# A fused decoder layer on one core: the last two modulation blocks move behind the attention pairs, and the page products start with the first pair

## The reference

```
mod = silu(c) @ w_ada + b_ada -> shift, scale, gate     (w_ada is 1024 x 3072)
h   = rms_norm(x) * (1 + scale) + shift
z   = h @ w_in                                          (1024 x 8200, 64 column tiles of 128)
A:  prompt: causal attention, 8 heads x 64, over z's q, k, v
    sample: 16 pages x 128 cached keys; mean key of each block of 2 pages,
            best 3 of 8 blocks by q . mean(k), softmax over those keys and the new one
B:  mLSTM, 4 heads, prompt and samples
u = sigmoid(ga) * (A * silu(za)) @ w_att + sigmoid(gm) * (B * silu(zm)) @ w_mlstm
y = rms_norm(x + gate * (u @ w_out))
```

## Time and profile before

| | |
|---|---|
| median of three runs | 740.91 us |
| the profiled execution | 738.85 us, its span 737.1 us |
| PE busy | 686.6 us, 93% |
| DVE busy | 480.9 us, 65% |
| POOL busy | 435.9 us, 59% |
| ACT busy | 333.4 us, 45% |
| mean granted TensorE clock | 0.973 of 2.4 GHz |
| loaded and stored | 144.72 MB, mean 196 GB/s |

### The profile page before, as it was taken

One profiled execution on the slowest core, in us unless ns is written; L12 is line 12 of the kernel. 1 busy time (PEld: TensorE's weight loads), 2 busy tenths in 40 slices (PEclk: granted clock), 3 DMA queues, 4 the chain that ended last, 5 costly groups with the idle time before them and its releaser, 6 DMA issues.

```text
span 737.1 us, 14735 instructions
## 1 busy us (share of the span) xinstructions
PE 686.6 (93%) x5012; PEld 610.7 (83%) x5012; DVE 480.9 (65%) x482; ACT 333.4 (45%) x727; POOL 435.9 (59%) x278
## 2 busy tenths in 40 slices
PE   2899999998998979999999999999899999999996
PEld 0575888786877948988999999997789998999974
DVE  0540689998999974895697687761665349444435
ACT  5544474646364325563464545612422224332643
POOL 4211257685686515899679688761495557666520
PEclk9998899999999988999999999999899999999999
DMA  8977858988798761286777567757548355732202
GB/s 315 343 269 233 242 177 244 280 256 270 231 305 262 222 220 29 70 253 198 226 212 228 186 197 238 215 180 207 140 114 228 100 154 174 238 109 85 87 25 92
DMA packets 156904, 144.72 MB, mean 196 GB/s; under 512 B 7547, under 2 KB 115152, under 8 KB 156852
## 3 DMA queue, kind: packets, MB, share of 16 engines
q1 hardware_dynamic: 142984, 137.15, 61.6%
q10 hardware_dynamic: 13876, 7.02, 3.1%
HBM read 135.10 MB, written 9.11 MB: 196 GB/s over the span
## 4 chain that ended last, share of the span: by engine, by line
PE 56%; DVE 16%; issue 10%; POOL 6%; SPq 5%; DMA 4%; ACT 3%; DVEq 0%; POOLq 0%; ACTq 0%
PE ps L553 39%; DVE sb_arenaA L1822 4%; PE ps L983 3%; POOL sb_wL L1507 3%; SPq L398 2%; DVE sb_arenaA L1969 2%; SPq L399 2%; POOL sb_arenaA L1553 2%; DVE sb_arenaA L1826 2%; POOL sb_arenaA L1585 1%; PE ps L822 1%; DMA sb_arenaA<-in_cache_k 1%; PE ps L783 1%; DVE sb_arenaB L1969 1%; DMA sb_arenaB<-in_x_sample 1%
## 5 line engine op out<-in xcount | busy, mean ns | idle before, releaser
L1507 POOL TENSOR_TENSOR sb_wL<-sb_wraw,sb_wH 128x512 fp32r<-128x512 f32 (+1 forms) x168 | 225.1, 1357 | 197.4 <-ACT sb_wH L1013 181.8
L553 PE MATMUL ps<-sb_hH,sb_wH 128*128 128x260 f32 x1152 | 240.6, 290 | 3.2 <-POOL sb_wL L1507 1.4
L553 PE MATMUL ps<-sb_hL,sb_wH 128*128 128x260 f32 x1152 | 234.2, 285 | 0.0
L553 PE MATMUL ps<-sb_hH,sb_wL 128*128 128x260 f32 x1152 | 233.8, 285 | 0.0
L553 PEld LDWEIGHTS ps<-sb_hH,sb_wH 128*128 128x128 f32 x1152 | 180.4, 192 | 15.8 <-issue 10.6
L553 PEld LDWEIGHTS ps<-sb_hL,sb_wH 128*128 128x128 f32 x1152 | 180.5, 191 | 0.0
L553 PEld LDWEIGHTS ps<-sb_hH,sb_wL 128*128 128x128 f32 x1152 | 179.7, 191 | 0.0
L1013 ACT ACTIVATE sb_wH<-sb_wraw 128x512 fp32r<-128x512 f32 (+1 forms) x168 | 98.7, 611 | 176.8 <-PE ps L553 145.8
L1585 POOL TENSOR_TENSOR sb_arenaA<-sb_arenaA 128x2048 f32<-128x2048 f32 x28 | 101.5, 3631 | 4.5 <-DMA sb_arenaA<-in_cache_v 2.5
L1826 DVE TENSOR_REDUCE sb_arenaA<-sb_arenaA 128x2048 f32 (+1 forms) x32 | 72.9, 2285 | 3.2 <-DVE sb_arenaA L1822 2.5
L1553 POOL TENSOR_TENSOR sb_arenaA<-sb_arenaA 128x2048 f32<-128x2048 f32 x11 | 56.5, 5138 | 26.0 <-DMA sb_arenaA<-in_cache_k 26.0
(11 more groups left out here) (390 smaller groups left out, 975.5 us busy)
## 6 DMA issues: line engine op xcount, KB each, us to landing
sb_wraw<-in_w_in SPq DMA_DIRECT2D x64, 512.0 KB, 5.3
sb_arenaA<-in_cache_k SPq DMA_DIRECT2D x128, 256.0 KB, 3.1
sb_arenaA<-in_cache_v SPq DMA_DIRECT2D x128, 256.0 KB, 3.2
sb_arenaA<-in_w_ada SPq DMA_DIRECT2D x6, 2048.0 KB, 12.0
sb_arenaB<-in_state_C SPq DMA_DIRECT2D x8, 512.0 KB, 3.9
sb_wraw<-in_w_mlstm SPq DMA_DIRECT2D x8, 512.0 KB, 4.8
sb_wraw<-in_w_out SPq DMA_DIRECT2D x8, 512.0 KB, 3.9
sb_arenaB<-in_x_prompt SPq DMA_DIRECT2D x1, 2048.0 KB
```

The lines of the kernel that those rows point to most:

```text
L553: last = mm(ps[:, 2 * s + a, 0:HALF], w[:, s, k, :], x[:, k, a * HALF:(a + 1) * HALF], start=(k == 0 and w is wH and x is xH), stop=(k == ...
L1507: tt(wL[:, j % 2, part], wraw[:, j % 4, part], wH[:, j % 2, part].bitcast(F32), ALU.subtract)\
```

## The change

Blocks 5 and 6 of the modulation leave the first attention pair: they are loaded when the last key steps have left their slots, and computed among tiles 3 to 5 of the mLSTM. The queries' block is computed before the gate logits. Both first queries are spread at once. The key pages start after the queries' block, all four pairs have the same eight steps (0 to 7 in DVE's own pair; three steps of a pair were done in the following one before), and POOL multiplies steps 0, 2 and 4 in place of 3, 7 and 5. `query_copy` and `copy_out` are one sample ahead, so that the second query of a pair is copied at the pair's start and the first one of the next at its end. The choice's first product stands inside tile 2, and the convolutions lie around the score work.

```diff
@ SP
-            for j in range(2, 4):
-                att_first(j)
-                ada_block(2 + j)
-            ada_block(6)
+            att_first(2)
+            ada_block(4)
+            att_first(3)
...
-            sp.wait_ge(ada_used, 7)
+            sp.wait_ge(ada_used, 5)
...
-                tile(0, n, following(0, tt_))
-                tile(1, n + 1, following(1, tt_))
-                for i, s in enumerate((0, 3, 2, 1, 4, 7, 5, 6)):
-                    if i in (2, 4):
-                        tile(1 + i // 2, n + 1 + i // 2, following(1 + i // 2, tt_))
-                    key_pages(s, t)
+                for what in ((1, 0, 2, 3, "t0", "t1", 4, "t2", 5, "t3", 6, 7) if first else
+                             ("t0", "t1", 0, 2, "t2", 1, 3, "t3", 4, 5, 6, 7)):
...
-            for j in (0, 1, 2, 3, "v0", "v1", 4, "v2", 5, "v3", 6, 7, "v4", "v5"):
+            for j in (0, "b5", 1, "b6", 2, 3, "v0", "v1", 4, "v2", 5, "v3", 6, 7, "v4", "v5"):
...
+                elif j[0] == "b":
+                    for s in range(2):
+                        sp.wait_ge(page_free[(2, 0)[j == "b6"] + s], 1 + 2 * PAIRS)
+                    ada_block(int(j[1]))
@ PE
             ztile(1, T_ATT + 1, hH, hL, parts=(0,))
+            pe.wait_ge(h_dve, 4)
+            pe.wait_ge(mod_rdy, 4)
+            modulation(W_Q, 7)
...
-            def qk(e, t):
+            def qk(e, t, first=False):
...
                     if e == 0 and b == 4:
-                        pe.wait_ge(qbc_rdy, 2 * t + 1)
+                        pe.wait_ge(qbc_rdy, 1 if first else 2 * t + 2)
...
                 if before:
                     ztile(0, n, hH, hL)
+                    pe.wait_ge(pnorm, 2 * t)
+                    ptrans(1)
+                    ztile(1, n + 1, hH, hL)
+                    pe.wait_ge(pt_ev, 2 * t + 1)
+                    query_copy(2 * t + 1, 1, 4)
+                    pv(1).then_inc(pv_done, 1)
                 else:
...
-                    modulation(5, 5)
...
-                    modulation(6, 4)
+                    ztile(1, n + 1, hH, hL, parts=(1,))
+                    pe.wait_ge(q_lo, 1)
+                    query_copy(0, 0, 4)
+                    query_copy(1, 1, 6)
...
-                    mod_turn(5, 1, 6, 0)
-                    mod_turn(6, 0, 6, 36)
-                    pe.wait_ge(q_lo, 1)
-                    pe.wait_ge(mod_rdy, 5)
-                pe.wait_ge(pt_ev, 2 * t + 1)
-                query_copy(0, t, 4)
-                if before:
-                    pv(1).then_inc(pv_done, 1)
...
-                query_copy(1, t, 7)
+                if not last_pair:
+                    query_copy(2 * t + 2, 0, 7)
                 qk(1, t)
-                pe.wait_ge(qbc_rdy, 2 * t + 2)
+                if not last_pair:
+                    pe.wait_ge(qbc_rdy, 2 * t + 3)
                 pv(0)
...
+            pe.wait_ge(sel_act, 1)
+            modulation(5, 6)
+            ztile(4, T_ML + 4, hH, hL)
+            pe.wait_ge(sel_dve, 4)
+            tr(ps[0:B * AH, 7, 0:P], mxA[:, :], ident[:, :]).then_inc(sel_pe, 1)
+            pe.wait_ge(ada_ev, 5)
+            modulation(6, 6)
+            ztile(5, T_ML + 5, hH, hL, parts=(0,))
+            pe.wait_ge(sel_dve, 5)
+            mm(ps[:, 7, 128:192], ones[0:B * AH, :], dg64[:, :], start=True, stop=True).then_inc(sel_pe, 1)
+            ztile(5, T_ML + 5, hH, hL, parts=(1,))
+            pe.wait_ge(ada_ev, 6)
+            mod_turn(5, 1, 6, 0)
+            mod_turn(6, 0, 6, 36)
@ ACT
-            def copy_out(e, t, before):
+            def copy_out(i, e, bank, before):
                 if before:
                     for slot in range(KV_SLOTS):
-                        act.wait_ge(page_free[slot], 2 * t + e)
-                act.wait_ge(qbc_mm, 2 * t + e + 1)
+                        act.wait_ge(page_free[slot], i)
+                act.wait_ge(qbc_mm, i + 1)
...
-                copy_out(0, t, before)
+                if before:
+                    copy_out(2 * t + 1, 1, 4, True)
...
-                copy_out(1, t, before)
+                if not last_pair:
+                    copy_out(2 * t + 2, 0, 7, True)
@ POOL
                 low(0, n + 4)
-                key_step(3, t)
+                key_step(4, t)
                 low(1, n + 5)
                 low(2, n + 6)
-                key_step(7, t)
+                if not last:
+                    key_step(0, t + 1)
                 low(3, n + 7)
                 if not last:
-                    key_step(5, t)
+                    key_step(2, t + 1)
@ DVE, attention(t, before)
                 if not before:
                     gates_in()
                     gate_sums()
-                    dve.wait_ge(t_mod, 6)
-                    bias_added(slice(16, 24), 6, 0).then_inc(mod_rdy, 1)
+                    key_step(1, t)
+                    gate_max()
                 causal_max(0, t)
-                if before:
-                    key_step(7, t - 1)
-                else:
-                    gate_max()
-                inverse_sums(0, t)
-                if before:
-                    key_step(6, t - 1)
-                    key_step(5, t - 1)
-                else:
+                if not before:
                     gate_stabilisers()
+                    inverse_sums(0, t)
+                key_step(0, t)
+                if before:
+                    inverse_sums(0, t)
+                    key_step(1, t)
+                else:
                     states_convolved()
-                key_step(0, t)
+                for s in (2, 3):
+                    key_step(s, t)
                 causal_max(1, t)
-                key_step(3, t)
+                key_step(4, t)
                 inverse_sums(1, t)
-                for s in (1, 2, 4):
+                for s in (6, 5, 7):
                     key_step(s, t)
                 output_gated(t)
@ DVE, after the pairs
-            for s in (7, 6, 5):
-                key_step(s, LAST)
```

121 lines of the change are left out of this document (66 added, 55 removed).

## The result

The changed kernel took 745.81 us (median of 20 runs, 742.41 to 754.19), the kernel before 741.29 us in the same series. The ratio is 1.0065, 95% interval [1.0045, 1.0084]: about 4.8 us slower. That lies between the two ends that the prediction names, 728 and 747, and within 1%, but on the other side of the forecast. The profiled execution has a span of 742.3 us against 737.1.

A forecast was written before the change was run, and what follows sets the result against it. PE was busy 93%, with DVE setting the pace in the pairs and SP near its limit. Gains of 2.1 and 1.3 us (choice) took 3.4 off 738.85, giving 735.4; plus 2.1 for the median, 737.5, range 728 to 747.

The forecast's parts named there:

- The queries' block, the first scores: First pair's start on PE: no wait for the queries' block, scores end at 66.1 instead of 74.5, pages from 47.9.
- The first pair: DVE's eight steps of the first pair end at 111.4 us; before, five were done by 116.3.
- The loop: Later pairs: 20.5 us from last sum to second maxima, rounds of 41.9 us through the query copies, against SP's 40.8.
- pv(1): Products with v after the last second maxima: forecast to end at 232.1 us, against 236.0 before.
- The choice: From 232.1 us to the end of the spread: 40.6 us including waits, end at 272.7 against 276.1; 1.3 us gained here.
- for as much: Ahead of the first head's tile: turning and waits may lower the clock, costing as much as the possible 1.6 us gain.
- 2.1 us gained: First term of the sum: the last second maxima start at 215.7 us instead of 217.83.
- Given back at once: Rival, 0.17: DVE's queue and new waits take the first pair's gain before 241, blocks cost 5.7 us; 741 to 743.
- blocked rival: Rival, 0.17: POOL's and DVE's products block each other in three rounds, 3.2 us each; 744, or 754 with both blocks.

The follow-up runs named there:

- e10: The changed kernel with the scan of the gate maxima reading one of its two inputs from the accumulator memory: 745.0 us, ratio 1.0047 to the kernel before.
- e2: The changed kernel with query copies released by the last product that reads the query, not by the sums: 744.6 us, ratio 1.0045 to the kernel before.
- e9: The kernel before without blocks 5 and 6 at all (not loaded, multiplied or turned): 742.3 us, ratio 1.0006 to the kernel before.
- e1: The changed kernel without blocks 5 and 6 at all (not loaded, multiplied or turned): 736.0 us, ratio 0.9917 to the kernel before.
- e4: The kernel before with only blocks 5 and 6 moved from the first pair into the choice, around the ranking's wait: 744.7 us, ratio 1.0051.
- e5: The changed kernel with both blocks back in the first pair and all pages after them: 743.5 us, ratio 1.0032 to the kernel before.
- e15: The changed kernel run again unaltered, as a control in another series: 748.8 us, ratio 1.0094 to the kernel before.

## Why the prediction was wrong

I forecast -3.4 us on the profiled execution and it was +5.2. The 8.6 us between them, by the steps of the prediction:

- **The queries' block, the first scores.** Right: no wait (start 45.48), scores end at 65.7 (forecast 66.1), the page start at 48.5 for 47.9.
- **The first pair: +2.7.** DVE's eighth sum ended at 114.1, not 111.4. The scan took 4.58 us for 1.21, beside POOL's product of step 2 (69.85 to 74.4), and step 6 waited 1.45 us for its page. I had drawn POOL's second product and the scan, and not laid them over each other. The scan alone doesn't explain the 2.7: in e10 it took 1.21 and the pair still ended at 113.5, behind first scores that ended 2.2 us later. I had also taken the low clock of the first pair to be covered; it came as before (0.88 from 54 to 97 us in both kernels).
- **The loop: +3.1.** 21.4 instead of 20.5 from there to the second maxima, and rounds of 43.0 instead of 41.9, twice. The waits are the ones that I named (query copies ahead of the last group and of `pv(0)`), 1 to 2.3 us each. e2 shows that they carry about 1 us of the round, and that pages and POOL are just behind. Both halves of the round were 0.5 to 0.9 us longer than drawn (114.07 to 135.49 and 157.47 to 178.50: 21.4 and 21.0 for 20.5; 135.49 to 157.47: 22.0 for 21.4). A stretch of 3.4 us at 1.2 GHz follows PE's stops in them, and I had assumed full clock.
- **pv(1)** then ends at 238.1, where I said 232.1: these two terms, and 0.2.
- **The choice: +2.6.** 43.2 us from there to the end of the spread, not 40.6. The ranking's wait went, as said, and block 5 was there in time. The waits were 3.5 as said. The clock was not: the first scores at 4.00 instead of 2.40. I had named it as "for as much", either way, and left it out. The other 1.0 us lies in the work terms, and no single row holds it.

The step that failed is the first term of the sum, "2.1 us gained" at the last second maxima (215.7 against 217.83). They stood at 221.52, 3.7 us behind the old place, because the first pair ended 2.7 us and the loop 3.1 us later than drawn; either of the two by itself takes the 2.1 away. The second term, the choice, was 2.6 us short, 1.6 of it for the low clock that I had left out. The waits that I named were the right ones; their surroundings were too cheap in every part, and nearly all the errors went one way.

Behind this lies a price that I never worked out: what the two blocks cost where they stood. I took them off PE by their rows (1.92, 1.92, 1.93 and a wait of 1.16) and didn't ask what the old order would do without them. e9 measures that price as -0.06% [-0.36, 0.24], with a wait of 2.76 us for the gates' logarithms in the place of the blocks; e1 measures it in the choice of the new order as 1.5% (0.9917 for 1.0065). In the choice I had 5.7 us of work and 2.7 of waits for them; there they cost 10.2. "Given back at once", which I gave 0.17 and 741 to 743, was nearest: the gain is given back, and the choice costs more than its 5.7.

One rival's price was added up wrongly. The blocked rival's 744 and 754 take the gain of 3.4 off twice, once in 737.5 and once by itself; from 740.9 they are 747 and 757.

The sum over the cases: without the blocks the new order is faster than the old one by 0.9% (e1, e9). With the blocks in the choice the new order is 0.65% slower than the kernel before and the old order 0.5% (e4). With them in the first pair the new order is slower by 0.3% (e5), since its pages then wait. Early pages and blocks in the first pair both want the same space, and in the choice nothing covers the blocks; that is why neither place gives the gain of e1.

What stays open: how much of the 4.8 us is clock. The mean granted clock over the timed executions was 0.964 in the changed kernel (0.962 in e15) and 0.967 to 0.969 in the one before, and within a kernel an execution with 0.01 more clock was 3 to 6 us shorter, so 1 to 3 us of the difference may be that; no run held the clock fixed. Open too is the split of the first pair's 2.7 us.

## What to carry to other kernels

Work that stands on the busiest engine may still be free: leave it out in its old place before paying for a new one. Here that is one run, and it would have shown that moving the blocks by themselves had nothing to win. Price a moved piece by its work, the waits of its own small chain (here product, copy, product, turning) and the clock behind them; here these made 10 us of 5.8. And where a gain needs two things that share a buffer (early pages, and blocks in the pages' space), count them as one choice: moving one block of the two, with the new scan and its copy issued earlier, was the only version with all of its work that came out ahead.
